# Eleven of eighteen modulation parts multiplied and summed over rows on GpSimd, and the filling work of the first attention laid evenly over its units

## The reference, cut to what matters

```python
mod_l = (silu_c @ mod_w[i] + mod_b[i])[:, None, :]
mod_c = silu_cc @ mod_w[i] + mod_b[i]
sh1, sc1, g1, sh2, sc2, g2 = jnp.split(mod_l, 6, axis=-1)
```

## Time and profile before

| | us |
|---|---|
| median of 3 runs (2490.41 to 2493.22) | 2492.98 |
| the profiled execution's own time | 2493.66 |
| its span, first to last instruction | 2491.8 |
| TensorE busy | 2380.9 |
| VectorE busy | 508.3 |
| ScalarE busy | 364.9 |
| GpSimd busy | 0.2 |

### The profile page before, as it was taken

The page is one execution under the profiler, slowest core; times in us unless marked ns, Lnnn a source line. Parts: engine busy times, 40 slices in busy tenths (PEclk is TensorE's granted clock), DMA queues, the critical chain, the costliest instruction groups (busy, mean ns, idle before and its releaser), DMA issues.

```text
span 2491.8 us, 27195 instructions
## 1 busy us (share of the span) xinstructions
PE 2380.9 (96%) x10738; PEld 1223.2 (49%) x10739; DVE 508.3 (20%) x1185; ACT 364.9 (15%) x764; POOL 0.2 (0%) x4
## 2 busy tenths in 40 slices
PE   6988899999999998999999989999999999999997
PEld 3454444444444476888888733333333333333333
DVE  1123312111100123211014221212112221211212
ACT  3112212100100221211024310000000000000001
POOL 0000000000000000000000000000000000000000
PEclk9999899999999999999999989999999999999999
DMA  9737414222122426644563349999986979999895
GB/s 383 271 120 280 141 54 132 84 68 76 64 80 84 148 72 220 203 148 140 169 203 119 136 198 418 418 418 418 418 342 277 413 319 402 418 418 418 350 418 218
DMA packets 211777, 602.61 MB, mean 242 GB/s; under 512 B 10370, under 2 KB 127362, under 8 KB 178690
## 3 DMA queue, kind: packets, MB, share of 16 engines
q1 hardware_dynamic: 209600, 599.04, 62.8%
q10 hardware_dynamic: 2114, 2.67, 0.3%
HBM read 600.62 MB, written 1.05 MB: 241 GB/s over the span
## 4 chain that ended last, share of the span: by engine, by line
PE 84%; DMA 7%; SPq 4%; DVE 2%; ACT 2%; issue 1%; DVEq 0%; ACTq 0%
PE bank L306 53%; PE bank L768 29%; DMA wring<-in_w_gu 6%; SPq L1762 4%; PE bank L793 1%; DMA wring<-in_ev_w_in 1%; ACT big L905 1%; ACT tmp L905 1%; DVE big L1296 0%; DVE big L1290 0%; PE bank L483 0%; DVE sm L1393 0%; DVE tmp L1290 0%; DVE big L1293 0%; DVE tmp L1296 0%
## 5 line engine op out<-in xcount | busy, mean ns | idle before, releaser
L768 PE MATMUL bank<-wring,big 128*64 128x512 f32 x3456 | 773.3, 596 | 26.3 <-DMA wring<-in_w_gu 16.5
L306 PE MATMUL bank<-hT,wring 128*128 128x256 f32 (+1 forms) x2240 | 723.0, 485 | 1.8 <-DMA wring<-in_ev_w_in 1.8
L306 PEld LDWEIGHTS bank<-hT,wring 128*128 128x128 f32 x2240 | 427.0, 192 | 292.8 <-issue 249.5
L768 PEld LDWEIGHTS bank<-wring,big 128*64 128x64 f32 x3456 | 235.6, 137 | 512.7 <-issue 443.3
L306 PE MATMUL bank<-big,wring 128*128 128x256 f32 (+1 forms) x1096 | 343.2, 475 | 6.3 <-DVE big L1293 3.6
L306 PEld LDWEIGHTS bank<-big,wring 128*128 128x128 f32 x1096 | 209.7, 192 | 139.5 <-issue 116.3
L905 ACT ACTIVATE big<-bank 128x256 f32<-128x256 f32 (+3 forms) x216 | 100.8, 467 | 813.6 <-PE bank L793 502.3
L1293 DVE TENSOR_SCALAR big<-bank 128x512 f32<-128x512 f32 (+1 forms) x73 | 50.0, 685 | 475.0 <-PE bank L768 474.6
L768 PE MATMUL bank<-big 64*128 64x256 f32 (+1 forms) x872 | 141.3, 463 | 0.5 <-ACT big L905 0.5
L768 PEld LDWEIGHTS bank<-big 64*128 64x128 f32 (+1 forms) x872 | 74.4, 171 | 76.9 <-issue 71.4
L1296 DVE SCALAR_TENSOR_TENSOR tmp<-bank,vecs,tmp 128x510 f32<-128x510 f32 (+1 forms) x88 | 54.2, 615 | 205.2 <-ACT tmp L905 203.6
(11 more groups left out here) (134 smaller groups left out, 946.3 us busy)
## 6 DMA issues: line engine op xcount, KB each, us to landing
wring<-in_w_gu SPq DMA_DIRECT2D x256, 1024.0 KB, 16.5
wring<-in_w_down SPq DMA_DIRECT2D x128, 1024.0 KB, 15.8
wring<-in_mod_w SPq DMA_DIRECT2D x48, 1024.0 KB, 12.0
wring<-in_ffn_w_up SPq DMA_DIRECT2D x44, 1024.0 KB, 5.1
wring<-in_w_ada SPq DMA_DIRECT2D x24, 1024.0 KB, 5.0
wring<-in_ffn_w_down SPq DMA_DIRECT2D x16, 1024.0 KB, 5.0
wring<-in_w_in SPq DMA_DIRECT2D x14, 1024.0 KB, 5.0
wring<-in_ev_w_in SPq DMA_DIRECT2D x12, 1024.0 KB, 12.1
```

What stands on the lines that cost most here:

```text
L306: ins = pe.matmul(o, l, r, start=start, stop=stop, skip_group_check=True)
L768: ins = pe.matmul(o, l, r, start=start, stop=stop, skip_group_check=True)
```

## The change

Eleven parts, (0,2) to (0,5), (1,0) to (1,4), (2,1) and (2,2), are no longer matmuls of their weights. SP loads their weights as 8 tiles of 128x1024 (0.5 MB) into three of the former ring slots (the ring has 9 for the stream before the experts, and 12 again from them on). GpSimd multiplies each tile by a column of `cs` for each condition, and adds the products up in `ACC`, one for each condition. TensorE then needs one product with a selector (`sel`, a column of ones) to sum over the 128 rows: `reduce`, 4 matmuls of 256 columns for each condition. The rest of the way (rows, transposes, bias) is as before. The 11 reductions stand in the attention's units 1 and 9, behind the attention, in FFN 0 at the steps 1, 3, 5, 7, 9, in the retention at head 1, and in FFN 1 at the steps 2 and 7. The eight tile loads of a part stand in SP's queue among the weight loads: those of part i behind slots 8 and 9 past its predecessor's reduction, each waiting for GpSimd to be through with the tile three before it. The first GpSimd operation of a part waits for the reduction of the part before.

In the qkv stage the head statistics take the banks 6 and 7 and the rotations 4 and 5. Of the v projection only the first half stands there; the second half's four tiles stand in the units 0 to 3 of the attention, and the twelve keys of the gate projections in the units 4 to 15, one in each. ScalarE and VectorE follow in order.

```diff
 RING = 12
+EARLY = 9
...
         IN_NORM = {1: (1, 5), 2: (2, 0), 3: (2, 3), 4: (2, 4)}
-        MOD_ORDER = [(m, part) for m in range(3) for part in range(6)]
+        SUMMED = [(0, 2), (0, 3), (0, 4), (0, 5), (1, 0), (1, 1), (1, 2), (1, 3), (1, 4), (2, 1), (2, 2)]
+        IN_ATT = {1: (0, 2), 9: (0, 3)}
+        IN_FFN = [{1: (0, 5), 3: (1, 0), 5: (1, 1), 7: (1, 2), 9: (1, 3)}, {2: (2, 1), 7: (2, 2)}]
+        FILL = {4 + 6 * pr + 2 * i + j: (part, 2 * pr + j) for pr in range(2) for i, part in enumerate((1, 2, 0))
+                for j in range(2)}
+        MODW = [wring[:, EARLY, 0:D], wring[:, EARLY, D:2 * D], wring[:, EARLY + 1, 0:D]]
+        PROD = wring[:, EARLY + 1, D:2 * D]
+        ACC = [wring[:, EARLY + 2, D * i:D * i + D] for i in range(2)]
+        def conditions(m, part):
+            return (2,) if m == 2 else (0, 1) if m == 0 or part < 2 else (0,)
+        summed = [0]
+        for m, part in SUMMED:
+            for t in range(8):
+                summed.append(summed[-1] + len(conditions(m, part)) * (2 if t else 1))
+        reduced_at = {}
...
+            def reduce(m, part):
+                i = SUMMED.index((m, part))
+                ws = conditions(m, part)
+                if i == 0:
+                    pe.wait_ge(G("sel_set"), 1)
+                pe.wait_ge(G("mod_acc"), summed[8 * i + 8])
+                bk, fl = claim(("mr", m, part), 7)
+                for x, w in enumerate(ws):
+                    last = x == len(ws) - 1
+                    for g in range(4):
+                        mm(bk[32 * g:32 * g + 32, 0:256], sel[:, 32 - w:64 - w], ACC[x][:, 256 * g:256 * g + 256],
+                           x == 0, last, fl if last and g == 3 else None)
+                reduced_at[i] = len(stream)
...
-                bk, fl = claim(("mod", m, part))
+                bk, fl = claim(("mod", m, part), 7 if (m, part) in SUMMED else None)
...
+                    if jj - 1 in IN_FFN[l]:
+                        turn_rows(*IN_FFN[l][jj - 1])
+                    if jj in IN_FFN[l]:
+                        reduce(*IN_FFN[l][jj])
...
                 pe.wait_ge(G("qk_norm"), c + 1)
-                bk, fl = claim(("rot", c))
...
                 qk_stat(2 * c2)
                 qk_stat(2 * c2 + 1)
-                modulation(0, 2 + c2)
-                if c2:
-                    turn_rows(0, 1 + c2)
-            project_rows("v0", win, 2560, 0, range(4))
-            turn_rows(0, 5)
+            project_rows("v0", win, 2560, 0, range(4), (0,))
             qk_rot(6)
             qk_rot(7)
...
-            gates = []
-            for pr in range(2):
-                for part in (1, 2, 0):
-                    gates.append(([("g", part, 2 * pr), ("g", part, 2 * pr + 1)], 512 * part + 256 * pr))
+            def fill(u, held):
+                ws = held.rearrange("p (k n) -> p k n", k=8)
+                if u < 4:
+                    bk, fl = claim(("v0", 1, u))
+                    for k in range(DC):
+                        mm(bk[:, 0:256], hT[:, k, P * u:P * u + P], ws[:, k, :], k == 0, k == DC - 1,
+                           fl if k == DC - 1 else None)
+                else:
+                    part, j = FILL[u]
+                    bk, fl = claim(("g", part, j))
+                    for k in range(DC):
+                        mm(bk[:, :], ws[:, k, P * (j % 2):P * (j % 2) + P], hT[:, k, :], k == 0, k == DC - 1,
+                           fl if k == DC - 1 else None)
             for u in range(len(UNITS) + 2):
                 if u < len(UNITS):
                     scores(u)
-                if u % 3 == 1 and gates:
-                    keys, c0 = gates.pop(0)
-                    project(keys, colsrc(win, c0), 0, T2)
-                if u in MOD_U:
-                    modulation(1, MOD_U.index(u))
-                if u - 1 in MOD_U:
-                    turn_rows(1, MOD_U.index(u - 1))
+                    if u == 0:
+                        held = slot(colsrc(win, 2560 + 256))
+                    elif u >= 4 and u % 2 == 0:
+                        part, j = FILL[u]
+                        held = slot(colsrc(win, 512 * part + P * j))
+                    fill(u, held)
+                    if u == 3 or (u >= 4 and u % 2):
+                        done()
+                if u in IN_ATT:
+                    reduce(*IN_ATT[u])
+                if u - 1 in IN_ATT:
+                    turn_rows(*IN_ATT[u - 1])
                 if 1 <= u <= len(UNITS):
                     turn_p(u - 1)
                 if u >= 2:
                     pv(u - 2)
-            for keys, c0 in gates:
-                project(keys, colsrc(win, c0), 0, T2)
+            reduce(0, 4)
...
                 if h == 1:
                     project([("rp", 0), ("rp", 1)], colsrc(win, 0), 2, S)
                     project([("rp", 2), ("rp", 3)], colsrc(win, 256), 2, S)
-                if h in (1, 2):
-                    modulation(2, h)
-                if h in (2, 3):
-                    turn_rows(2, h - 1)
+                if h == 1:
+                    reduce(1, 4)
+                if h == 2:
+                    turn_rows(1, 4)
                 if h:
                     ret_out(h - 1)
...
             base = len(stream)
-            MOE["slot0"] = base
+            MOE["place"] = [(EARLY + i, 0) for i in range(3)] + [((base + i) % EARLY, (base + i) // EARLY) for i in range(EARLY)]
             def wslot(s, e):
-                n = base + s
-                pe.wait_ge(w_full[n % RING], e * 16 + 16 * (n // RING + 1))
-                return wring[:, n % RING, :]
+                i, uses = MOE["place"][s]
+                pe.wait_ge(w_full[i], e * 16 + 16 * (uses + 1))
+                return wring[:, i, :]
...
-                if u in (5, 7):
-                    modulation(2, u // 2 - 1)
+                if u == 5:
+                    modulation(1, 4)
...
+        @block.gpsimd
+        def _(pool):
+            pool.wait_ge(G("cond"), 1)
+            for i, (m, part) in enumerate(SUMMED):
+                if i:
+                    full(pool, ("mr", *SUMMED[i - 1]))
+                for t in range(8):
+                    n = 8 * i + t
+                    ws = conditions(m, part)
+                    pool.wait_ge(G(f"modw_in{n % 3}"), 16 * (n // 3 + 1))
+                    for x, w in enumerate(ws):
+                        to = ACC[x] if t == 0 else PROD if x < len(ws) - 1 else MODW[n % 3]
+                        if t and x < len(ws) - 1:
+                            pool.wait_ge(G("mod_acc"), summed[n])
+                        pool.tensor_scalar(to, MODW[n % 3], cs[:, t, w:w + 1], None, ALU.mult).then_inc(G("mod_acc"), 1)
+                    if t:
+                        pool.wait_ge(G("mod_acc"), summed[n] + len(ws))
+                        for x in range(len(ws)):
+                            pool.tensor_tensor(ACC[x], ACC[x], PROD if x < len(ws) - 1 else MODW[n % 3],
+                                               ALU.add).then_inc(G("mod_acc"), 1)
         @block.sync
         def _(sp):
             sp.dma_start(xT[:, :, :], xin).then_inc(G("x_loaded"), 16)
-            n0 = MOE["slot0"]
-            def load(n, src, w):
-                sp.dma_start(wring[:, n % RING, 0:w] if len(src.shape) == 2 else
-                             wring[:, n % RING, 0:w].rearrange("p (k n) -> p k n", k=src.shape[1]),
-                             src).then_inc(w_full[n % RING], 16)
+            def load(i, src, w):
+                sp.dma_start(wring[:, i, 0:w] if len(src.shape) == 2 else
+                             wring[:, i, 0:w].rearrange("p (k n) -> p k n", k=src.shape[1]),
+                             src).then_inc(w_full[i], 16)
+            def load_mod(n):
+                i, t = n // 8, n % 8
+                m, part = SUMMED[i]
+                if n >= 3:
+                    sp.wait_ge(G("mod_acc"), summed[n - 2])
+                w = (mod_w[0], mod_w[1], w_ada[0])[m].rearrange("(p t) n -> p t n", t=8)
+                sp.dma_start(MODW[n % 3], w[:, t, D * part:D * part + D]).then_inc(G(f"modw_in{n % 3}"), 16)
+            beside = {}
+            for i in range(len(SUMMED)):
+                for t in range(8):
+                    n = reduced_at[i - 1] + EARLY - 1 + t // 4 if i else EARLY + t // 2
+                    beside.setdefault(n, []).append(8 * i + t)
             for n, (src, w) in enumerate(stream):
-                if n >= RING:
-                    sp.wait_ge(w_used, n - RING + 1)
-                load(n, src, w)
+                if n >= EARLY:
+                    sp.wait_ge(w_used, n - EARLY + 1)
+                load(n % EARLY, src, w)
+                for k in beside.get(n, ()):
+                    load_mod(k)
             def expert(s, e):
                 if s < GUC:
                     return w_gu[0, e, P * s:P * s + P, :]
                 return w_down[0, e, 256 * (s - GUC):256 * (s - GUC) + 256, :].rearrange("(j p) n -> p j n", p=P)
-            for s in range(RING):
```

(28 more changed lines are left out.)

82 lines of the change are left out of this document (44 added, 38 removed).

## The result

The change made the kernel slower: 2571.43 us, median of 4 runs (2570.54 to 2572.37), against 2493.10 (2490.41 to 2494.73, 4 runs) for the kernel before. The ratio is 1.0314, with a 95% interval of 1.0301 to 1.0327. The forecast of 2448 and its range (2424 to 2490) both missed. What came is the rival "GpSimd becomes the bound", near its upper end (2578 at T = 82). The profiled execution took 2570.54, its span 2568.5.

What follows compares the result with a forecast made beforehand. TensorE was taken to bound the kernel, busy 96% of the span. Of 68 us won, 9 and 4 of lateness and 10 of contention came off: 45 us from 2493.66, forecast 2448 us, range 2424 to 2490.

Steps and rivals of the forecast that it cites:

- GpSimd becomes the bound: Rival, chance 0.13: four tight places wait for GpSimd; above 61 us per two-condition part the 68 us gain is eaten.
- T: GpSimd's time for a two-condition part, 16 multiplications and 14 additions of 128x1024; forecast 48 us.
- The failed step: GpSimd's price in the summed parts: multiplication 1.1 us, addition 2.0, 0.2 for each of 14 waits on itself; 48 us together.
- The upper bound, 82: GpSimd's two-condition part priced from above: 30 operations at 2.73 us, VectorE's scan scaled to 1024 columns.
- The tight places: Reductions of (0,3), (0,4) in the attention, forecast 9 and 4 us late; (1,0), (1,1) in FFN 0, just covered.
- the 8 us that I had added to each part in the attention: GpSimd meeting VectorE's work on the same memory in the attention: 0 to 13 us, taken as 8.
- 68 us with the cover untouched: TensorE's gain if GpSimd is in time: 43.5 + 9.0 + 18.7 + 5 - 7.8 us.
- The qkv stage of 82 us: Qkv stage after the change, with four modulation parts and its waits for VectorE gone: 82 us long.
- 3 us waits: Qkv stage: three waits of 3.00 us for VectorE to free a common-ring bank go, 9.0 us won.
- units of 9.0 us: Attention: each unit takes 7.0 us of filling plus about 2.0 of its own work.
- The ring of 9 slots and SP's queue at nothing: Weight stream: cutting the ring from 12 to 9 and tile loads waiting in SP's queue cost nothing.
- Contention in the retention: (2,1) summed beside VectorE's chain: TensorE stands 21 us more if in series, 0 if beside; 10 taken.

Runs made afterwards that it cites:

- 64-column: Changed kernel with GpSimd working on only 64 of each tile's 1024 columns behind a part's first tile: 2390.91 us, ratio 0.9598; fewer expert matmuls.
- 536-column kernel: Changed kernel with GpSimd working on 536 of each tile's 1024 columns behind a part's first tile: 2429.63 us in one run.

## Why the prediction was wrong, point by point

- **The failed step: "I take the multiplication at its own row (1.1) and the addition ... in the middle of its ends (2.0)", so T = 48.** VectorE's rows are no price for GpSimd. Measured: 2.87 and 2.36, and T = 80.7. Of the 33 us missing, 16 x 1.77 = 28 are the multiplication's and 14 x 0.36 = 5 the addition's. The upper bound, 82, was almost exact, and the multiplication even lies above its own (2.73). I took both from the side nearer to VectorE because no row priced the engine, which is a reason for a wide range and not for a low value. The 64-column and the 536-column kernel show that this step makes the miss: without it the change wins.
- **The tight places** were named rightly. By the prediction's slacks with T = 81 they come to (5 + 81 - 52) + (5 + 81 - 57) + 2 x (5 + 81 - 56) = 123 us late; measured 33.4 + 28.0 + 31.2 + 28.1 = 120.7. This leaves out the 8 us that I had added to each part in the attention for GpSimd's waits for VectorE. They were too many: those two parts take 80.7 and 80.4 us, (1,0) and (1,1) in the FFN 79.9 and 79.6.
- **The price beside the waits.** I had left out the clock. The attention ran at 0.83, and the matmuls of a reduction behind a wait took 1.8 times as long (1.93 for 1.07). With no waits at all (64 columns) the same stage is 137.8 long, with the 61.4 of waits 211.6. So 12 us come on top. TensorE's busy time in the stage is 145.9 where it is 137.9 with 64 columns and a clock of 1.00, so 8 of them are matmuls that ran longer. The other 4.5 are waits for VectorE, 3.45 of them in one piece at 123.68, which the kernel with 64 columns does not have.
- **68 us with the cover untouched:** 71.1. The qkv stage of 82 us: 81.8. No 3 us waits there; units of 9.0 us (with 64 columns): right. TensorE's busy time fell by only 28 us, not by the 43.5 - 7.8 = 36 of the parts; matmuls that ran longer at the lower clock took the rest. The ring of 9 slots and SP's queue at nothing: TensorE's waits for weights ahead of the experts come to 2.0 us, in two pieces, the last ahead of the first q projection.
- **Contention in the retention, "I take 10".** The chain of 32 instructions went from 13.0 to 21.8 us, so 8.8. Neither 0 nor 21: VectorE is held by some of GpSimd's instructions for all of their length and by others for a part. Timelines of the changed kernel, VectorE above, GpSimd below:

```profile
1035.21 2.48 DVE L1543 COPY tmp<-tmp 128x254 f32<-128x254 f32 x1
1037.61 0.16 DVE L1544 COPY tmp<-tmp 128x2 f32<-128x2 f32 x1
1037.80 1.14 DVE L1347 TENSOR_TENSOR tmp<-tmp 128x253 f32<-128x253 f32 x1
1038.98 0.43 DVE L1347 TENSOR_TENSOR tmp<-tmp,xT 128x256 f32<-128x256 f32 x1
1039.44 0.42 DVE L1347 TENSOR_TENSOR big<-tmp,big 128x256 f32<-128x256 f32 x1
1039.78 0.68 DVE L1542 TENSOR_TENSOR_SCAN tmp<-tabs,big 128x256 f32<-128x256 f32 x1
1040.50 2.47 DVE L1543 COPY tmp<-tmp 128x252 f32<-128x252 f32 x1
```

```profile
1035.20 2.34 POOL L1835 TENSOR_TENSOR wring<-wring 128x1024 f32<-128x1024 f32 x1
1037.52 2.88 POOL L1831 TENSOR_SCALAR wring<-wring,cs 128x1024 f32<-128x1024 f32 x1
1040.48 2.34 POOL L1835 TENSOR_TENSOR wring<-wring 128x1024 f32<-128x1024 f32 x1
```

A copy of 0.29 us that meets an addition takes 2.48 and ends just behind it. Under the multiplication that follows, after a copy of two columns, a product (1.14 in place of 0.42) ends 1.4 us into it. It was held until 1.0 us into it, then, and the next three instructions run at full speed beside the rest of it. Products that read a PSUM bank keep their 692 ns.

The rest of a multiplication isn't free for every form. In the attention of the changed kernel VectorE's tensor_scalar of two columns, SBUF to SBUF, which takes 0.17 elsewhere, begins 1.9 us into a multiplication and ends with it (VectorE, then GpSimd, two multiplications of which the second is meant):

```profile
187.29 0.95 DVE L1350 TENSOR_SCALAR sm<-sm 128x2 f32<-128x2 f32 x1
```

```profile
182.27 5.96 POOL L1831 TENSOR_SCALAR wring<-wring,cs 128x1024 f32<-128x1024 f32 x2 [0.17 <-POOL wring L1835]
```

The Trainium skill (SBUF — State Buffer, "Who interferes with whom") speaks of an exclusive lock, which the one that issues first gets for the whole instruction. The runs agree for tensor_tensor (2.48 for 0.29; products of 1933 ns beside multiplications of 1961). They don't for tensor_scalar, where VectorE's products run at full speed from 1.4 us into the instruction on. The Trainium skill (GPSIMD Engine Reference, section 3.1) has 4497 ns for an addition of 2048 columns; half of it, 2.25 us, is an estimate for 1024, and 2.36 was measured. The Trainium skill's rule in section 4.1 of the same page, that one-input operations go roughly at line rate, was wrong here: 2.87 measured. The estimate from its figures was T = 47, as wrong as that from VectorE's rows; the measurement decides.

- **The chances.** I gave 0.13 to GpSimd as the bound, though the stretch from 61 (where the gain is eaten) to the upper bound of 82 was nearly half of the range of T, and four places in a row depended on the one number. With an unpriced engine, T spread evenly from 35 to 82 gives that rival (82 - 61) / 47 = 0.45.

## What to carry to other kernels

Price work for an engine by an instruction measured on that engine, in that form and size. Where there is none, spread the chance over both bounds, and ask at which value the sign turns. Put the point at which a background engine's result is wanted one measured duration and some reserve after its start: with the same GpSimd instructions the kernel is 78 us slower than before in one placing and 50 faster in another. Measure the halves of a change apart, too: of those 50 us, 34 needed nothing of GpSimd. A shorter form can cost more than a longer one if it holds the neighbour for its whole length, so read the neighbour's durations by form before and after.

## What the runs showed of the hardware that I had not expected

- On GpSimd a multiplication of 128x1024 f32 by a column takes 2.87 us, by a constant 2.79, and as a tensor_tensor with a broadcast column 1.93; an addition of two full tiles takes 2.36. Both forms with one full operand are slower than both tensor_tensor forms.
- A copy or a product of VectorE out of SBUF that begins under a tensor_tensor of GpSimd ends just behind it (2.48 us for a copy of 0.29). Under a tensor_scalar of 2.88 a product is held until 1.0 us into it, and those begun from 1.4 us on run at full speed (0.43). A tensor_scalar of VectorE begun at 1.9 us is held up to the end (0.95 for 0.17). Instructions with an operand in PSUM are not held (692 ns).
- A dependent instruction of GpSimd starts 0.17 us after the one it waits for.
